# Six modulation tiles of the second layer between the pieces of the joint attention

## The reference

```python
silu_c, silu_cc = silu(c), silu(c_ctx)
for l in range(2):
    mod_l = silu_c @ w_ada[l] + b_ada[l]          # 6 x 1024: sh1, sc1, g1, sh2, sc2, g2
    mod_c = silu_cc @ w_ada[l] + b_ada[l]
    h = rmsnorm(x, norm_mix[l]) * (1 + sc1) + sh1  # of both streams
    o = mixer_ab(h) if l == 0 else mixer_na(h)     # joint attention; neighbourhood attention
    x = x + g1 * o
    h = rmsnorm(x, norm_ffn[l]) * (1 + sc2) + sh2
    x = x + g2 * hier_moe(h)                       # 32 experts, two of a group of 8 for each row
```

## Time and profile before

| | |
|---|---|
| three timed runs | 2997.81, 2999.63, 3007.0 us (median 2999.63) |
| profiled execution | 2997.95 us, span 2996.0 us |
| PE busy | 2883.8 us, 96% |
| DVE, ACT, POOL busy | 1025.0, 562.4, 179.0 us |
| HBM read, written | 700.37, 11.76 MB |
| mean granted clock | 0.993 |

### The profile page before, as it was taken

One profiled execution on the slowest core, in us unless ns is written; L12 is line 12 of the kernel. 1 busy time (PEld: TensorE's weight loads), 2 busy tenths in 40 slices (PEclk: granted clock), 3 DMA queues, 4 the chain that ended last, 5 costly groups with the idle time before them and its releaser, 6 DMA issues. The chain is left out here.

```text
span 2996.0 us, 34497 instructions
## 1 busy us (share of the span) xinstructions
PE 2883.8 (96%) x14167; PEld 1664.3 (56%) x14167; DVE 1025.0 (34%) x2664; ACT 562.4 (19%) x1302; POOL 179.0 (6%) x300
## 2 busy tenths in 40 slices
PE   7999999999999999999999999999978989999998
PEld 4576547864468555884556555454434455444443
DVE  3444523421444532541435432222222064222222
ACT  1322411100231421211155110000011051000000
POOL 0000041000000000000000010000012021000000
PEclk9999999999999999999999999999989999999999
DMA  5457647354256545543040379999984227999996
GB/s 213 141 177 252 225 137 249 121 182 145 86 176 243 210 163 202 204 150 108 23 155 5 146 293 428 428 428 427 428 354 149 82 64 275 410 428 427 427 428 266
DMA packets 183445, 708.18 MB, mean 236 GB/s; under 512 B 16563, under 2 KB 25859, under 8 KB 156017
## 3 DMA queue, kind: packets, MB, share of 16 engines
q1 hardware_dynamic: 166624, 668.56, 57.2%
q0 software_dynamic: 16368, 37.32, 3.8%
q10 hardware_dynamic: 288, 0.01, 0.0%
HBM read 700.37 MB, written 11.76 MB: 238 GB/s over the span
## 5 line engine op out<-in xcount | busy, mean ns | idle before, releaser
L643 PE MATMUL bank<-h1T,wslot 128*128 128x256 f32 x2176 | 473.7, 380 | 2.2 <-issue 2.2
L643 PEld LDWEIGHTS bank<-h1T,wslot 128*128 128x128 f32 x2176 | 412.1, 190 | 61.4 <-issue 6.0
L2713 PE MATMUL bank<-wslot,xgT 128*64 128x512 f32 x672 | 296.7, 596 | 6.8 <-DMA another<-in_moe_w_up 2.6
L2730 DVE TENSOR_TENSOR hid<-gs,bank 64x512 f32<-64x512 f32 x65 | 68.6, 1056 | 467.4 <-ACT gs L2724 467.4
L2714 PE MATMUL bank<-wslot,xgT 128*64 128x512 f32 x512 | 226.0, 594 | 0.0
L2685 PEld LDWEIGHTS bank<-sel,hT 128*128 128x128 f32 x1600 | 182.9, 193 | 23.7 <-issue 23.5
L2685 PE MATMUL bank<-sel,hT 128*128 128x128 f32 x1600 | 188.8, 278 | 0.0
L2724 ACT ACTIVATE gs<-bank 64x512 f32<-64x512 f32 x65 | 38.4, 591 | 580.1 <-PE bank L2714 580.1
L2713 PEld LDWEIGHTS bank<-wslot,xgT 128*64 128x64 f32 x672 | 90.7, 137 | 97.8 <-issue 97.8
L506 PE MATMUL bank<-wslot,hT 128*128 128x512 f32 (+3 forms) x320 | 110.1, 498 | 9.0 <-DVE hT L2060 4.1
L2805 PE MATMUL bank<-wslot,aT 128*64 128x512 f32 x336 | 113.3, 595 | 0.0
(11 more groups left out here) (461 smaller groups left out, 4118.8 us busy)
## 6 DMA issues: line engine op xcount, KB each, us to landing
wslot<-in_moe_w_gate SPq DMA_DIRECT2D x41, 2048.0 KB, 18.9
wslot<-in_moe_w_down SPq DMA_DIRECT2D x38, 2048.0 KB, 19.8
wslot<-in_w_in SPq DMA_DIRECT2D x36, 2048.0 KB, 9.3
wslot<-in_moe_w_up SPq DMA_DIRECT2D x32, 2048.0 KB, 15.2
wslot<-in_w_ada SPq DMA_DIRECT2D x24, 2048.0 KB, 8.7
wslot<-in_ffn_w_up SPq DMA_DIRECT2D x20, 2048.0 KB, 8.9
late<-in_moe_w_gate SPq DMA_DIRECT2D x13, 2048.0 KB, 18.7
extra<-in_moe_w_up SPq DMA_DIRECT2D x13, 2048.0 KB, 15.8
```

What stands on the lines that cost most here:

```text
L643: ins = pe.matmul(b.t[:, 0:width], w[:, k, j * P:(j + 1) * P], xT(k), start=(k == 0), stop=(k == kc - 1))
L2713: pe.matmul(bk.t[other, :], xt.t[:, k, mine], wg[:, j, :], start=(k == 0), stop=(k == KD - 1))
L2730: K.mv = K.dve.mark(v.tensor_tensor(a_.t[mine, :].rearrange("p (k q) -> p q k", k=DE // P), g_.t[mine, :].rearrange("p (q k) -> p q k", k= ...
```

## The change

Six tiles of the modulation's second layer, 4, 5, 6, 7, 10 and 11, are taken from the plan and the steps of the first block and put between the projections and the output projection of the joint attention. Their steps go to the rounds 5, 10, 15, 20, 25 and 30 of the attention's pipeline, ahead of all else in the round, and use the two banks of the transposes. The conditioning vector is made a second time at the start of the second block, and the six pieces of bias are loaded in 24 small transfers. The two gate rows of the joint attention's output projection are loaded behind the attention, row 1 (the context's) and then row 0.

```diff
+BESIDE_JOINT = (4, 5, 6, 7, 10, 11)
+
+
+def ada_here(l, j):
+
+    return l == 0 or j not in BESIDE_JOINT
@@ plan_first @@
         if name == "ada":
-            ada(i)
+            if ada_here(l, i):
+                ada(i)
...
     for j in (8, 9, 10):
-        ada(j)
+        if ada_here(l, j):
+            ada(j)
...
-        if j == 0:
+        if j == 0 and ada_here(l, 11):
             ada(11)
@@ first_ssd, beside @@
                 for j in (4 + 2 * n, 5 + 2 * n):
-                    yield from ada.steps(j)
+                    if ada_here(l, j):
+                        ada.step(j)
+                    yield
+def conditioning(K, silu, spread):
+
+    @K.block.scalar
+    def _(act):
+        for due in K.due(act, K.fetched, *K.settled):
+            act.wait_ge(*due)
+        K.ml = K.act.mark(act.activation(silu[:, :], K.early[:, 0:2 * KD], ACT.Silu).then_inc(K.act.sem, 1))
+
+    @K.block.vector
+    def _(v):
+        for due in K.due(v, K.ml, *K.settled):
+            v.wait_ge(*due)
+        K.mv = K.dve.mark(v.tensor_copy(
+            spread[:, :, :].rearrange("p k (a s) -> p k a s", s=2),
+            silu[:, :].rearrange("p (k s) -> p k s", s=2).unsqueeze(2).broadcast_to([P, KD, COLS // 2, 2]))
+            .then_inc(K.dve.sem, 1))
+    return spread, K.mv
@@ class Modulation @@
-    def step(self, j):
+    def step(self, j, banks=None, at=None):
         K, n = self.K, P // COLS
         i, w, landed = K.take(("ada", self.l, j))
-        b, r = K.banks.next(), self.rows.next()
+        b, r, at = (banks or K.banks).next(), self.rows.next(), j % 8 if at is None else at
...
-            K.mv = K.dve.mark(v.tensor_tensor(r.t[:, :], b.t[:, 0:P], self.bias[:, j % 8, :], ALU.add)
+            K.mv = K.dve.mark(v.tensor_tensor(r.t[:, :], b.t[:, 0:P], self.bias[:, at, :], ALU.add)
                               .then_inc(K.dve.sem, 1))
...
+    def later(self, ctx):
+
+
+        K, l = self.K, 1
+        self.l, self.loaded = l, []
+        silu, spread = K.sb("silu_c", [P, 2 * KD], ctx=ctx), K.sb("silu_spread", [P, KD, COLS], ctx=ctx)
+        self.silu_c = conditioning(K, silu, spread)
+
+        @K.block.gpsimd
+        def _(g):
+            for at, j in enumerate(BESIDE_JOINT):
+                src = K.A["b_ada_2"][l, 512 * j:512 * j + 512].rearrange("(q c) -> q c", c=P)
+                for q in range(P // COLS):
+                    self.loaded.append(K.move(g, self.bias[COLS * q:COLS * (q + 1), at, :], src[q].partition_broadcast(COLS),
+                                              *K.settled))
+
+    def beside(self, banks):
+
+        for at, j in enumerate(BESIDE_JOINT):
+            self.step(j, banks, at)
+            yield
+
+    def written(self):
+
+        return [m for r in self.rows.bufs for m in r.free]
@@ first_ffn @@
-        ada.step(10)
+        if ada_here(l, 10):
+            ada.step(10)
...
-                ada.step(11)
+                if ada_here(l, 11):
+                    ada.step(11)
@@ plan_second @@
             K.plan_tile(("kvup", n), A["mla_w_kv_up_2"][0], 0, KVL // P, 512 * n, 512)
+        for j in BESIDE_JOINT:
+            K.plan_tile(("ada", 1, j), A["w_ada_2"][1], 0, KD, 512 * j, 512)
@@ joint_attention @@
-        fetch_gate((K.pe, K.pe.count))
...
-        pipeline(jobs, 7)
+        pipeline(jobs, 7, ada.beside(w["turned"]), 5)
         K.noted()
+        K.settled = [*K.settled, *ada.written()]
     return done
@@ second_block @@
             return place
         with ExitStack() as c2:
             oT = late[:, :].rearrange("p (k n) -> p k n", k=KD)
-            g1 = [K.sb(f"g1{s}", [P, D], ctx=c2)[:, :] for s in range(2)]
-            gm = []
-
-            def fetch_gates(read):
-                @K.block.gpsimd
-                def _(g):
-                    for s, row in enumerate(g1):
-                        gm.append(K.move(g, row, modrows[0, MG1, s].partition_broadcast(P), read))
-            attended = joint_attention(K, hT, S.ready, oT, cols, rowt, fetch_gates)
+            with ExitStack() as c3:
+                ada = Modulation(K, c3, modrows)
+                ada.later(c3)
+                attended = joint_attention(K, hT, S.ready, oT, cols, rowt, ada)
+            g1, gm = [K.sb(f"g1{s}", [P, D], ctx=c2)[:, :] for s in range(2)], []
+
+            @K.block.gpsimd
+            def _(g):
+                for s, row in reversed(list(enumerate(g1))):
+                    gm.append(K.move(g, row, modrows[0, MG1, s].partition_broadcast(P), *K.settled))
             place = another(0)
             M.load_rows(c2)
             projected = add_gated(K, c2, x_of, [("abo", 0), ("abo", 1)], lambda k, t: oT[:, k, t * P:(t + 1) * P],
```

More of the change, by code:

```diff
@@ L2079, in first_block @@
         rowt = second.rowt
[L2081 to L2097, removed]
         ada = Modulation(K, ctx, modrows)
@@ L2113, in first_block @@
                 second.load(colt)
-                ada.silu_c = conditioning()
+                ada.silu_c = conditioning(K, silu, spread)
                 after = lambda k, t: colt[:, PCW + PC["norm_mix"] + k:PCW + PC["norm_mix"] + k + 1]
@@ L2253, in add_gated, with joint_attention @@
             yield
-def joint_attention(K, hT, hready, oT, cols, rowt, fetch_gate):
+def joint_attention(K, hT, hready, oT, cols, rowt, ada):
     block = K.block
```

## The result

The changed kernel takes 3007.86 us (median of 6 runs, 3006.72 to 3014.89), the kernel before 3002.32 beside it (6 runs). The ratio is 1.0027, 95% interval 1.0016 to 1.0037: slower by 5 to 11 us. Measured again in five rounds it is 1.0032 (1.0020 to 1.0045). The time is inside the forecast's range of 2995 to 3010, but it can be told from no change, and the forecast's sum of +3.4 us is less than half of the 8 us that the ratio gives.

What follows compares the result with a forecast made beforehand. The prediction took TensorE, busy 2883.8 of 2996.0 us, to bound the kernel. Its terms, -9.5 + 10.2 + 0.4 + 2.3 = +3.4 us, gave 3003.0 us as the median, range 2995 to 3010.

Steps and rivals of the forecast that it cites:

- The experts and all behind them: Expert tiles loaded during the attention arrive in time: no cost, and TensorE's delay is carried to the end one for one.
- A step in the attention: Each moved tile costs TensorE 1.6 us in rounds 5 to 20, 1.88 in rounds 25 and 30; 10.2 us lost.
- The pay-back: Rival in the attention: later rounds' waits vanish, so each step costs 0.5 us; 2995.8 us in all; chance 0.15.
- the lost round: Rival in the attention: each step costs a whole round, 16.7 us for six; 3009.5 us in all; chance 0.10.
- Gate rows: Behind the attention, the gate rows delay the routing loads by 2.6 us, leaving TensorE idle 2.3 us.
- Half rate: Rival at the gate rows: loaded at half the rate, they cost 4.6 us instead of 2.3; 3005.3 us; chance 0.10.
- The old place: First block: removing five tiles gains 1.88 us each, tile 10 only some 0.1; 9.5 us gained together.
- The start: Joint block's start: remaking the conditioning vector, with two table loads on ScalarE, costs 0.4 us.
- DMA relief: Rival at the old place: busy DMA hides late tiles, so removing six loads gains 29 us; 2974 us; chance 0.05.

Runs made afterwards that it cites:

- loads24: Kernel before plus 24 small bias loads that nobody reads, on GpSimd's queue at the joint block's start; ratio to before 1.0009.
- bias8: Changed kernel with the six pieces of bias loaded in 8 transfers instead of 24; ratio to the kernel before 1.0028.
- filler: Kernel before with one extra 128x128 matmul on constants ahead of L934 in ten attention rounds; one profiled execution, no time measured.
- late_gates: Kernel before with only the two gate rows loaded behind the attention, ahead of the six routing row loads; ratio to before 1.0021.
- rows_first: Changed kernel with the six routing rows loaded ahead of the gate rows, first two tiles waiting for the first gate row alone; ratio to before 1.0019.
- after_again: The changed kernel itself, unaltered, measured once more; ratio to the kernel before 1.0032.
- after_warm: Changed kernel with independent matmuls on constants put into five idles of TensorE; ratio to the kernel before 1.0036.
- mended: Changed kernel with bias in 8 transfers, gate rows loaded behind the routing rows, and steps in rounds 3, 6, ..., 18; ratio to before 1.0008.
- ps_fill: Kernel before with modulation tile 7 of both layers moved ahead of the ps projection, where TensorE waits; ratio to before 0.9986.
- in_waits: Against before: tile 7 of both layers ahead of ps, second-layer tiles 5, 6, 11 in joint projections' waits, gate rows early; 2991.11 us, ratio 0.9973.

## Why the prediction was wrong, step by step

- **The experts and all behind them: the step that failed.** "The same loads follow the same matmuls, so a delay of TensorE is carried to the end one for one", and the 24 bias loads "go out while it has nothing else": both counted GpSimd's loads as time on a queue alone. They also count as transfers. GpSimd pauses at its 234th, and with 24 more that is the last write of expert rows: its wait went from 3.76 to 6.32 us, TensorE's at L661 from 13.8 to 16.2: 2.5 us, priced at nothing. loads24 and bias8 show that the number of loads does it, the fourteen traces that the pause goes by the number of the transfer. Why GpSimd pauses there stays open.
- **A step in the attention: 1.88, not 1.6.** The mechanism was right, the size off by 0.28 us in four steps, 1.1 us. I took the 0.33 us ahead of L934 for waiting, on the name of VectorE in its bracket. filler shows that it is not free, and the steps' own records stand behind the same 0.33. The Trainium skill (TensorEngine Tiling (Array Packing), Tiling Modes, Key Properties) says that a change of tiling mode drains TensorE; with that the prediction bounded the step at 1.88, and the gaps of 0.20 and 0.33 us where the shape changes agree with it. The pay-back and the lost round were wrong: each step cost 1.8 to 1.9 wherever TensorE was not waiting, three or five rounds apart.
- **Gate rows: 2.7, not 2.3.** The wait for the loads was 3.0 us longer, not 2.6. The chain from VectorE's gain rows to the transposes was as forecast. Half rate was wrong. late_gates and rows_first show it from both sides.
- **The old place: right, slightly small.** -10.0 against -9.5; the tiles measured 1.94 to 2.08 us, 0.06 to 0.2 over the 1.88 of the timeline. Tile 10 gave nothing, as said. **The start:** 0.56 against 0.4. **DMA relief:** none.
- **The clock: not priced, and not settled.** Low-clock time is twice (1 - mean clock) times the span. In the profiles of before it is 42 us, of after 49; over runs of the same call 46 against 54 for after_again. At half speed 8 us of it are at most 4. Part of it is in the profile: the step of round 5 took 2.39 us, not 1.95, in a stretch of 3.4 us at a granted clock of 0.50, 1.2 GHz (windows of after, below), that came right behind an idle of 1.7 us; before has idles of 1.9 and 2.8 us ahead of 1436 and 1493 without one. But after_warm filled such idles and kept its 54 us, and mended, with the same six tiles moved, has 49 against 46. The other way round, the profiles of late_gates, filler and ps_fill, with no tile in the attention, each have three such stretches between 1428 and 1553 us, where before and loads24 have none. So it isn't a fixed price of the moved tiles; what sets it stays open.

```profile
1536.00:1541.40 5.40, 2.58 (x18) 1.32 (x16) 1.51 (x4) 4.66 (x12) 0.00 (x0) 1.00 0.75 257
1541.40:1544.80 3.40, 3.40 (x31) 2.10 (x32) 1.15 (x4) 1.69 (x7) 0.00 (x0) 0.50 0.57 216
```

All errors but the old place's had one sign: 2.5 + 1.1 + 0.4, less 0.5 at the old place, plus 0.2 at the start, make 3.7, and lead from +3.4 to +7.1. The measured +5 to +11 us holds that; what is left of it may be the clock's. The chances called everything within 0.3% no change, while the comparison resolves about 0.1%: with a forecast of +3.4 and terms that could each grow, slower deserved much more than 0.11.

## What to carry to other kernels

A piece of work is free only where the engine in question waits for another and none of its own order follows behind: the same tiles cost 1.88 us each in a pipeline that looked half idle on all other engines, and nothing at five waits of 1.6 to 2.8 us. Read a gap in front of an instruction against the gap of its neighbours before calling it a wait. And a transfer that hides in time can still cost something where it is only counted: number the transfers of a queue in both traces, and look at the same number as well as at the same instruction, however far from the change.

## What was not expected of the hardware

- GpSimd's 234th transfer started 1.3 to 2.6 us late in all fourteen profiles, be it a small load, a large one or a write. Twenty-four small loads put that pause onto a write 800 us later, where it cost 2.56 us, the same in all six profiles with 24.
- One more 128x128 matmul on constants cost 0.2 us ahead of L934 in rounds of 256 keys and 0.42 in rounds of 512, while its records last 0.39.
- A tile's 64 records, 1.95 us from the first start to the last end, gave back up to 2.08 us where it was removed.
- The mean time at the lower clock was 46 to 48 us in each group for before, 48 or 49 for loads24, ps_fill and mended, 51 for in_waits, which is the fastest, and 52 to 60 for the seven others timed over rounds.
